# Splitting the output weights in the first attention tile, regrouping the output jobs, and reordering the first loads of a hybrid streaming layer on one Trainium2 core

## The reference, cut to what matters

```python
hn = _rmsnorm(h, attn_norm)                 # 1024 columns
z = hn @ w_in                               # the combined input projection
cq, ckv_pre, kr_pre, hq, hf, hi, hg = jnp.split(z, ...)
...                                         # latent attention (8 heads) and gated recurrence (4 heads)
h = h + jnp.concatenate([o_mla, o_hg], axis=-1) @ w_o     # w_o is 1024 x 1024
h = h + _hier_moe(_rmsnorm(h, ffn_norm), ...)
```

## Time and profile before

| what | value |
|---|---|
| median of three executions | 1324.56 us |
| the profiled execution, its own time | 1328.77 us |
| its span in the profile | 1327.0 us |
| mean granted TensorE clock | 0.927 of full |
| first phase | 0 to about 290 us |
| second phase | about 290 to 885 us |
| third phase | about 885 us to the end |
| HBM read, written | 234.92 MB, 48.94 MB |

### The profile page before, as it was taken

The page is one execution under the profiler, slowest core; times in us unless marked ns, Lnnn a source line. Parts: engine busy times, 40 slices in busy tenths (PEclk is TensorE's granted clock), DMA queues, the critical chain, the costliest instruction groups (busy, mean ns, idle before and its releaser), DMA issues.

```text
span 1327.0 us, 18397 instructions
## 1 busy us (share of the span) xinstructions
PE 1113.3 (84%) x5855; PEld 895.7 (67%) x5855; DVE 733.5 (55%) x1336; ACT 520.5 (39%) x935; POOL 370.2 (28%) x370
## 2 busy tenths in 40 slices
PE   3999999969976889899899999954898988988920
PEld 3889899945564777677777776743676767777720
DVE  3430510156665566556464654437786877787837
ACT  4333222123332222222222322304776777777712
POOL 2100500001053111101010101103665656656556
PEclk9999999979987989899989998975999999999975
DMA  6340141152058566574535452904788786764576
GB/s 244 109 148 0 57 132 47 46 128 65 7 206 297 199 207 214 183 252 145 191 143 190 144 175 89 329 34 150 265 270 297 253 276 231 256 224 180 186 266 233
DMA packets 104596, 234.44 MB, mean 177 GB/s; under 512 B 15104, under 2 KB 63696, under 8 KB 95312
## 3 DMA queue, kind: packets, MB, share of 16 engines
q1 hardware_dynamic: 81264, 117.68, 26.0%
q0 software_dynamic: 22176, 113.78, 24.6%
q10 hardware_dynamic: 1088, 2.10, 0.5%
HBM read 234.92 MB, written 48.94 MB: 214 GB/s over the span
## 4 chain that ended last, share of the span: by engine, by line
PE 54%; DVE 11%; DMA 10%; issue 10%; ACT 8%; POOL 4%; SPq 2%; POOLq 1%; ACTq 0%; DVEq 0%
DMA below<-in_w 6%; PE ps L1013 4%; PE ps L903 4%; PE ps L2060 4%; PE ps L2062 4%; PE ps L2061 4%; PE ps L885 3%; DVE low L1737 3%; PE ps L972 3%; ACT high L1452 3%; PE ps L1054 3%; PE ps L1055 2%; PE ps L1056 2%; PE ps L2055 2%; PE ps L2054 2%
## 5 line engine op out<-in xcount | busy, mean ns | idle before, releaser
L1737 DVE TENSOR_TENSOR low<-below,high 128x1024 fp32r<-128x1024 f32 x128 | 193.7, 1560 | 75.2 <-ACT high L1452 65.6
L1415 POOL TENSOR_TENSOR low<-below,high 128x1024 fp32r<-128x1024 f32 x64 | 146.4, 2305 | 108.1 <-ACT high L1473 108.1
L1550 PE MATMUL ps<-high 128*128 128x512 f32 x384 | 156.2, 407 | 15.7 <-DVE low L1747 11.4
L1552 PE MATMUL ps<-high,low 128*128 128x512 f32 x384 | 151.4, 394 | 0.0
L1551 PE MATMUL ps<-low,high 128*128 128x512 f32 x384 | 151.2, 394 | 0.0
L1452 ACT ACTIVATE high<-below 128x1024 fp32r<-128x1024 f32 x128 | 129.5, 1052 | 43.6 <-DMA below<-in_w 43.0
L618 ACT ACTIVATE arena<-ps 128x512 f32<-128x512 f32 (+8 forms) x100 | 51.7, 527 | 201.4 <-PE ps L885 200.9
L885 PE MATMUL ps<-arena 128*128 128x128 f32 (+4 forms) x613 | 96.9, 283 | 12.5 <-ACT arena L865 4.4
L1918 POOL TENSOR_SCALAR arena<-arena 128x1 f32<-128x1 f32 (+5 forms) x38 | 14.0, 367 | 306.1 <-ACT arena L843 131.3
L1550 PEld LDWEIGHTS ps<-high 128*128 128x128 f32 x384 | 73.0, 190 | 36.3 <-issue 19.0
L769 POOL DMA_DIRECT2D high<-wo_dram x30 | 16.4, 547 | 284.7 <-PE ps L1056 268.2
(11 more groups left out here) (228 smaller groups left out, 2290.6 us busy)
## 6 DMA issues: line engine op xcount, KB each, us to landing
below<-in_w SPq DMA_DIRECT2D x256, 256.0 KB
high<-wo_dram POOLq DMA_DIRECT2D x32, 1024.0 KB, 5.3
low<-wo_dram POOLq DMA_DIRECT2D x32, 1024.0 KB, 7.4
below<-in_w POOLq DMA_DIRECT2D x64, 512.0 KB
y_dram<-arena SPq DMA_DIRECT2D x32, 512.0 KB, 3.1
arena<-in_x_prompt SPq DMA_DIRECT2D x16, 512.0 KB
below<-in_w_in SPq DMA_DIRECT2D x12, 512.0 KB, 6.7
out<-arena SPq DMA_DIRECT2D x9, 512.0 KB, 4.5
```

Of the source, the lines that this page charges most:

```text
L1415: pool.tensor_tensor(w2_lo[s % UN][:, c], w2_in[:, c], w2_hi[s % UN][:, c].bitcast(F32), ALU.subtract).then_inc(s_w2lo, 1)
L1550: pe.matmul(out, x_hi, w_hi, start=start, stop=False)
L1552: return pe.matmul(out, x_lo, w_hi, start=False, stop=stop)
L1737: dve.tensor_tensor(chunk(w13_lo[j], c), chunk(w13_in, c), chunk(w13_hi[j], c).bitcast(F32), ALU.subtract).then_inc(s_w13lo, 1)
```

## The change

1. **Weights split wholly in tile 0.** Two `ws` chunks stand at the end of each of the eight heads of tile 0. All four quarters are stored before the first output job, and every tile, tile 1 too, fetches its quarters. To make room, `ckv_t` moves from the `low` side's first floats to where the residual rows are kept later; so the residual rows of the first two tiles are loaded only once the last `kn` and `v` jobs are done.
2. **Output jobs in heads 3, 4, 5 and 7** in every tile (before: 2, 3, 5, 7, and 2 to 5 in tile 8). `sq` and `hn` of tile 8 stand where those of the other tiles do.
3. **The front.** The first rows of x are loaded in two halves of 64 partitions, one from SP's queue and one from ACT's, right at the front; the norm weights come next on ACT's queue; the first weight group comes half from each queue. PE multiplies tile 0 before it transposes tile 1, and ACT and DVE make the halves of tile 0 before those of tile 1.

```diff
-    r = Region(below_floats)
-    ckv_t = r.take(T + PAST)
+    r = Region(below_floats + KC * 512)
...
+    ckv_t = Region(r.at).take(T + PAST)
     h_row = r.take(2, D)
...
-    WO_AT = [{2: 0, 3: 1, 5: 2, 7: 3}] * (NT - 1) + [{2: 0, 3: 1, 4: 2, 5: 3}]
+    WO_AT = {3: 0, 4: 1, 5: 2, 7: 3}
...
-            if i == 1 and hd in WO_SPLIT_AT:
-                STEPS += wo_split(*WO_SPLIT_AT[hd])
+            if i == 0:
+                STEPS += wo_split(hd // 2, range(hd % 2 * 2, hd % 2 * 2 + 2))
...
-        store_wo(0)
-        store_wo(1)
+        for q in range(4):
+            store_wo(q)
+        sp.wait_ge(s_sps2, max(S_JOB[st] for st in STEPS if st[0] in ("kn", "v")) + 1)
+        load_residual(0)
+        load_residual(1)
+        sp.dma_start(fn_b, ffn_norm[0:1, :].to_broadcast([P, D])).then_inc(s_fn, 16)
...
             if kind == "wo":
-                n = 4 * i + hd + 2
-                if 4 <= n < 4 * NT - 2:
-                    load_wo(n // 4, n % 4)
+                if 4 * i + hd + 2 < 4 * NT - 2:
+                    pool.wait_ge(s_sps2, S_JOB[st] + 1)
+                    load_wo((hd + 2) % 4)
+            if st == ("attn", 0, MH - 1):
+                for q in range(2):
+                    pool.wait_ge(s_wost[q], 64)
+                    load_wo(q)
...
-                if i == 0:
-                    pe.wait_ge(s_wolo, 4 * hd + 4)
-                elif i + 1 == NT and hd >= 2:
+                if i + 1 == NT and hd >= 2:
                     pe.wait_ge(s_wo_last, 64)
                 else:
-                    pe.wait_ge(s_woin[hd % 2], 32 * (2 * (i - 1) + hd // 2 + 1))
+                    pe.wait_ge(s_woin[hd % 2], 32 * (2 * i + hd // 2 + 1))
...
+        sp.dma_start(tab[:, C_HALF:C_END], table[:, C_HALF:C_END]).then_inc(s_tab0, 16)
+        sp.dma_start(x_row[0:64, 0, :], x_prompt[0, 0:64, :]).then_inc(s_xrow[0], 16)
         sp.dma_start(tab[:, C_ID:C_ID + P], table[:, C_ID:C_ID + P]).then_inc(s_tab0, 16)
-        sp.dma_start(tab[:, C_HALF:C_END], table[:, C_HALF:C_END]).then_inc(s_tab0, 16)
...
-        load_x(0)
-        sp.dma_start(an_b, attn_norm[0:1, :].to_broadcast([P, D])).then_inc(s_norm_w, 16)
+        for c in (1, 3):
+            sp.dma_start(w_raw[:, 0, 2 * c:2 * c + 2, :], w_rows(0, c)).then_inc(s_wraw[0][c], 16)
...
-        for c in range(4):
+        act.dma_start(x_row[64:P, 0, :], x_prompt[0, 64:P, :]).then_inc(s_xrow[0], 16)
+        act.dma_start(an_b, attn_norm[0:1, :].to_broadcast([P, D])).then_inc(s_norm_w, 16)
+        for c in (0, 2):
             act.dma_start(w_raw[:, 0, 2 * c:2 * c + 2, :], w_rows(0, c)).then_inc(s_wraw[0][c], 16)
...
-        split_hi(act, 0)
-        square(1)
+        split_hi(act, 0, range(3))
         x_high(0)
+        square(1)
+        split_hi(act, 0, range(3, 4))
...
         x_turn(0)
-        for t in range(1, NT):
+        z_product(0, lambda: x_turn(1))
+        for t in range(2, NT):
             x_turn(t)
             z_product(t - 1)
...
         split_lo(dve, 0, 0, s_wlov)
+        x_low(0)
         split_lo(dve, 0, 2, s_wlov)
         x_scale(1)
-        x_low(0)
```

More of the change, by code:

```diff
@@ L452, in hybrid_layer @@
                 STEPS.append(("v", hd, 0))
-            side = ({1: "wot"} if i + 1 < NT else {1: "wot", 6: "sq", 7: "hn"}).get(hd)
+            side = {1: "wot"}.get(hd)
             if hd == 0:
@@ L457, in hybrid_layer @@
                 STEPS.append((side, i - 1, 0))
-            if i and hd in WO_AT[i]:
-                STEPS.append(("wo", i - 1, WO_AT[i][hd]))
+            if i and hd in WO_AT:
+                STEPS.append(("wo", i - 1, WO_AT[hd]))
             if hd == 6 and i + 1 < NT:
@@ L465, in hybrid_layer @@
                 STEPS.append(("attn", i, hd - 2))
[L466 to L467 removed]
+            if i == 0:
+                STEPS += wo_split(hd // 2, range(hd % 2 * 2, hd % 2 * 2 + 2))
         STEPS.append(("attn", i, 6))
[L469 removed]
+        if i:
             STEPS.append(("sq", i - 1, 0))
         STEPS.append(("attn", i, 7))
[L472 to L474 removed]
+        if i:
             STEPS.append(("hn", i - 1, 0))
@@ L482, in hybrid_layer @@
             STEPS.append(("ho", i + 1, 0))
-            if i == 0:
-                STEPS += wo_split(0, range(2, 4))
             STEPS.append(("qt", i + 1, 0))
@@ L763, in load_raw, with load_wo @@
                            w_o[0, kc * P:(kc + 1) * P, half * 512:(half + 1) * 512]).then_inc(s_woraw[c], 16)
-        def load_wo(i, q):
-            pool.wait_ge(s_sps2, S_JOB[("wo", i, q - 2) if q >= 2 else ("wo", i - 1, q + 2)] + 1)
-            if i == 1 and q < 2:
-                pool.wait_ge(s_wost[q], 64)
+        def load_wo(q):
             pool.dma_start(wo_hi[:, q % 2], wo_dram[0, q]).then_inc(s_woin[q % 2], 16)
@@ L819, in attention_act @@
                     act.wait_ge(s_wost[q % 2], 32)
-                    act.wait_ge(s_sps2, S_JOB[("wo", 0, q - 2)] + 1)
-                else:
-                    act.wait_ge(s_sps2, max(S_JOB[s_] for s_ in STEPS if s_[0] in ("kn", "v")) + 1)
                 act.activation(wo_hi[:, q % 2, c, :], wo_raw[:, c, :], ACT.Copy).then_inc(s_wohi, 1)
@@ L1817, in lo_done, with split_hi @@
         return 2 + 4 * g
-    def split_hi(act, g):
+    def split_hi(act, g, chunks=range(4)):
         n = GROUPS[g][2]
@@ L1825, in split_hi @@
             act.wait_ge(s_zps, Z_FIRST[g - 1])
-        for c in range(4):
+        for c in chunks:
             act.wait_ge(s_wraw[g % 2][c], 16 * (g // 2 + 1))
@@ L2045, in z_product @@
                 c = kc // 2
+                if between and kc == 6:
+                    between()
                 if n == Z_FIRST[g] and kc % 2 == 0:
```

18 lines of the change are left out of this document (3 added, 15 removed).

## The result

The changed kernel takes 1343.34 us (median of 4, 1338.04 to 1346.39), the kernel before 1325.38 us beside it: a ratio of 1.012 with a 95% interval of 1.008 to 1.016. It is slower by some 16 to 18 us. The forecast was 1315.5 us and faster, with a range that ended at 1327: sign and range were both wrong. The profiled execution of the changed kernel took 1338.04 us (span 1336.2), against 1328.77 before. It is the fastest of its four, and 1328.77 is slower than each of the four behind 1325.38, so the traces show 9.3 us of a loss that is 18 between the medians.

What follows compares the result with a forecast made beforehand. PE, busy 84% of the span, was taken as the bound, with time won only at its waits or lower clock. Terms -7.5 + 3 - 1 - 11.6 + 10.5 - 2.5 = -9.1 us gave a median of 1315.5 us, range 1303 to 1327.

Steps and rivals of the forecast that it cites:

- front: Start of the kernel: first product near 13.5 us, third transposes at 22.9 instead of 30.4; -7.5 us.
- tile 0: Tile 0: DVE instructions stand still beside POOL's low parts, in five of eight heads; +3 us, bounds 0 and 17.
- into tile 1: Passage from tile 0 to 1: without two high parts ahead on ACT, the copy of turned queries comes earlier; -1 us.
- tile 1: Tile 1: the wait for POOL's low parts and half clock go, a fetch comes in; -11.6 us, bounds -15 and -7.
- last tile: Tile 8: other work fills the 2.70 us wait and the half clock goes; -2.5 us, bounds -4 and 0.
- rest: The rest of the first phase and the whole third phase: same instructions and waits, counted at nothing.
- Head 2 of the tiles 2 to 7: Tiles 2 to 7: PE waits bare for a recurrence level; with fetches and +3 for clock, +10.5 us, bounds +3 and +18.
- rival D: Tiles 1 to 7: every longer idle stretch costs a half-clock spell; 14 us in place of 3, 1326.5 us; chance 0.08.
- rival A: Tile 0: every POOL low part holds DVE and PE back; 17 us in place of 3, 1329.5 us; chance 0.05.
- Rival B: Front: half rows land no sooner than the whole did, at 8.3 us; -3 instead of -7.5, 1320.0 us; chance 0.12.
- Rival C: Tiles 2 to 7: head 2's waits of 8.1 us vanish without a successor; sum -26.0, 1298.6 us; chance 0.10.

Runs made afterwards that it cites:

- e1: The kernel before with only the new front (part 3); output weights and jobs as before: 1319.28 us, ratio 0.996.
- e5: e4 with POOL's 16 low parts of the output weights replaced by memsets, so the result lacks them: 1303.40 us, ratio 0.984.
- e2: The kernel before with only the output weights split wholly in tile 0 and every tile fetching (part 1): 1321.58 us, ratio 0.997.
- e4: The whole change with output jobs back at heads 2, 3, 5 and 7 (2 to 5 in the last tile): 1309.88 us, ratio 0.989.
- e3: The kernel before with only the output jobs moved to heads 3, 4, 5 and 7 in all tiles (part 2): 1348.96 us, ratio 1.016.
- e6: The whole change with the turn of the mixed rows in head 0 instead of head 1: 1321.32 us, ratio 0.996.
- e11: The whole change with two extra matmuls behind the scores of head 2 in tiles 2 to 7, results unchanged: 1328.67 us, ratio 1.002.
- e9: The whole change with the turn of the mixed rows still in head 1, but behind the step of the recurrence: 1316.43 us, ratio 0.991.

## Why the prediction was wrong

Right by place, wrong by size, and the sizes were wrong in one direction. Terms of the sum against the profiled executions of before and after, and what of each was PE's busy time. PE's instructions are the same, so I take a change of its busy time as one of the clock:

| step | forecast | measured | busy time: forecast | measured | shown by |
|---|---|---|---|---|---|
| front | -7.5 | -6.3 at the third transposes, -5.8 at tile 0 | 0 | -0.3 | e1 |
| tile 0, with "into tile 1" | +2 | +8.0 | 0 | +4.1 | e5 |
| tile 1 | -11.6 | -7.9 | -4.9 | -2.3 | e2, e4 |
| tiles 2 to 7 | +10.5 | +14.0 | +3 | +9.2 | e3, e4, e6, e11 |
| last tile | -2.5 | -1.7 | -1.6 | -0.9 | |
| rest | 0 | +2.6 | 0 | +1.6 | |
| sum of the spans | -9.1 | +9.2 | -3.5 | +11.5 | |

**The clock was the step that failed.** "Head 2 of the tiles 2 to 7" gave it 3 us, "two more of 1.6"; in tile 0 it stood at nothing, and in tile 1 and the last tile I had only taken half clock away. In sum that was -3.5 us, and it measured +11.5: 15.0 of the 18.3 us by which the sum of the spans is off. The idle time, -5.6 by forecast and -2.3 measured, has the other 3.3.

In the tiles 2 to 7 the clock's part was 9.2 us against before, and the idle part 4.8 where I had 5.8 + 1.7 = 7.5. That the total of 14.0 lies near the forecast of 10.5 is luck: the two parts miss in opposite directions. Against e4, which differs in the job places alone, the same tiles have 6.9 us more of idle time and 12.3 more of busy time, and tile 1 has 4.5 (45.15 against 40.62). The two references differ because the kernel before has half-clock spells of its own, and more or fewer of them from one profiled execution to the next (324.8 to 332.8 us of busy time for the same work in before, e1 and e2).

This is the mechanism of rival D, to which I gave 0.08: its 14 us for the tiles 1 to 7 lie between the 6.9 us that the busy time there rose against before and the 16.8 against e4. I had a row for each kind of wait: the job at clock 1.00 after 1.46 us of idle, and at 0.61 after 2.70. The change turns the five waits of 1.44 to 1.86 us into five of 2.30 to 3.24 (in tile 3 it stayed at 1.10, where 2.6 or more was forecast), and these were to be priced by the second row, in every such tile, and over what follows the wait and not over one job: the spell of tile 5 lasted for more than 6 us. The wait itself was read well, 2.74 us for 2.6 in tile 5.

**Tile 0** was rival A's mechanism at half its price. The DVE instructions that stand still are those of the earlier trace rows, seven of them. But I counted only the delay on PE's path in one head and called four others like it. Idle time rose by 3.9 us against before (7.4 to 11.3) and is 5.0 above e5; the lower clock, again not counted, cost 4.1. Both bounds (0 and 17) held, the value chosen did not. What "into tile 1" was worth by itself no run shows.

**Tile 1**: the wait for POOL's low parts went, the fetch cost 2.4 us in the job of head 5 (forecast 2.1; in tile 2 it cost 0.9, forecast 1.4). With the jobs at their old heads the same tile takes 47.5 us (e4) or 50.7 (e2), with them at 3, 4, 5, 7 it takes 54.6 to 54.9 (after, e6, e9, e11). The split alone wins 11.8 us (e2); the forecast of -11.6 had the fetch and 1.1 us for head 2 in it as well, which leaves too little for the moved jobs. e6 and e9 have it at 54.9 and 54.8 too, so the late level is not all of it; what holds tile 1 at that length in them was not taken apart further than the fetch and a clock of 0.78.

**The front** was right to 1.2 us. The weights, not the rows, were late: chunks at 9.79 and 11.31. The rows landed by 5.97, for which I took 5. Rival B (nothing sooner than 8.3) fell. Whether the two half rows went one after the other no run shows alone.

**The last tile** fell by 1.7 us. But e4, with the old places, had 74.6 us, and e1 78.0 with the same order in that tile, so one execution cannot tell this from a difference of clock.

**The rest of the span**, counted at nothing, lay between 445.2 and 453.4 us over all the kernels here, whose instructions there are the same. The change's 449.5, and the 4.3 us of the 32.7 between it and e4, fall within that, and are not explained.

**Rival C** fell: the wait went over to the level, just as argued.

**The range** ended at 1327, for the far end of D as priced from before. I had treated the stalls in tile 0 (A) and the spell behind every long wait (D) as rivals, with each alone in place of the forecast. They are not alternatives, they add. With tile 0 at +8.0, tile 1 at -7.9 and the tiles 2 to 7 at +14.0 the sum goes from -9.1 to +4.1; the front (1.7 less won), the last tile (0.8) and the rest (2.6) bring it to the +9.2 of the traces. The medians are further apart than that: 1343.34 is 27.8 us above the forecast of 1315.5. Of the 9.5 us that the traces do not show, 5.3 are the distance of the changed kernel's traced execution from its median (the other three had granted clocks of 0.909 to 0.916, this one 0.919), and 4.2 are what I had taken off for that of the kernel before.

## What to carry to other kernels

Where PE's wait gets longer than those after which the trace shows it at full clock, price it as the wait plus the half-clock work behind it, once per repetition; here the second part was the larger one (12.3 against 6.9 us between e4 and the change). And count half clock wherever a stage gets more idle time, not only where it goes away. When a piece of PE work is moved away from in front of a wait, look at what stands ahead in the queue of the engine that ends that wait: moving the low half behind the level (e9) gave back 27 of the 33 us that moving the jobs had cost. And try the parts of a change apart: two of the three were gains, and together without the third they gave the kernel 14.6 us.
